# First block: the second transpose of the retention result moved ahead of one branch product, in a single-core fp32 two-block kernel

## The chip, the cores and the metric

One core of a Trainium2 chip (trn2) runs the whole program once. The metric is the device time of that execution in microseconds (us). A core has TensorE (PE, matrix products), VectorE (DVE), ScalarE (ACT), GpSimd (POOL) and SyncE (SP), which here only issues transfers. Each engine works through its own instruction list in order; they meet at semaphores.

## The reference, cut to what matters

Two blocks, one after the other, each of two layers, over 256 tokens of width 1024. The first block's layer:

```python
h = rms_norm(x, norm_g)
proj = h @ w_in                       # 8704 columns
a = diff_attention(...) * silu(az)    # branch 0, 512 wide
c = short_conv(...)     * silu(cz)    # branch 1
r = retention(...)      * silu(rz)    # branch 2
merged = sum(g[:, :, i] * (branches[i] @ w_branch[i]) for i in range(3))
x = x + merged @ w_out
```

The second block (feed-forward, a mixer with two attentions and a delta rule, feed-forward, twice) is in the program too, but the change leaves its order alone.

## The kernel before, in words

**Precision.** All large products are fp32 in effect. A weight piece of 128 x 2048 values (1 MB) is parted in a high and a low half: ACT copies `ring` to `ring_high` (line 1797), then DVE writes the rest, `ring` minus `ring_high`, as `ring_low` (line 2110). The activations are parted in the same way. PE then multiplies high by high, high by low and low by high (`in_parts`, lines 1162 to 1164), so each tile costs three matmuls.

**Rooms.** A loaded piece goes to one of four slots of `ring`, its high half to one of three slots of `ring_high`. A piece can be parted only once it has landed and PE is done with the piece that had its `ring_high` slot before. The transfers depend on the `ring` slots alone.

**Order.** `STEPS1` is the list of steps of a layer of the first block. Every engine takes the steps in which it has a part, in this order. ("d", o) is a product of the input projection. ("br", i, jp) is a quarter of the product of branch i (24 matmuls of 256 columns). ("RF2", t) is, on DVE, the last two operations on the retention result of token tile t (scale, then times silu), and `o_done` tells of it. ("RFT", t) turns it: PE waits for `o_done`, transposes four 128 x 128 tiles into bank 6, and ACT reads them out to `rT`. ("bs", 2) parts `rT` in a high half (ACT) and a low half (DVE, `scratch_low`, 128x1024), and the first product of branch 2 waits for the low half:

```python
                    if jp == 0:
                        pe.wait_ge(*branch_low(L, BRANCH_TURN[i]))
                    arrived(L, piece)
```

Projection and branch products take banks 0 to 3 in turn. After each branch product DVE multiplies the bank with the gate (line 2113); for branch 0 POOL adds that to the sum `hT` (line 2695), for branch 2 DVE does. ("ms", jp) parts a quarter of the merged sum, high half on ACT, low half on DVE (`hT_low`, 128x512). ("wo", q) for q = 0, 1 and then ("wl", i, a) are the output product: "wo" pieces 0 and 1 are used whole (24 matmuls of 512 columns each), pieces 2 and 3 by four quarters i, piece 2 + a by ("wl", i, a). ("wl", 0, 0) waits for the low half of "wo" piece 2 and of the merged quarter 2, ("wl", 0, 1) for those of piece 3 and quarter 3. The ("wl", ...) steps are interleaved with the start of the next layer.

**The planner.** The class `Plan` gives each piece its slots and puts the ("split", piece) steps into the list, at the earliest step behind which its slot is free. Slots go round in turn, but one of three must be skipped once, so that the turn ends where it began. Where the skip lies is chosen by a score: the sum over all pieces of 1 over the number of list positions between the freeing of the slot and its next use, rounded to one decimal; of equals the first in its list of ways is taken. The score changes when any step of the list moves.

Of the kernel before, what the change touches and what calls it, by code (L numbers as in the profile page):

```python
# [106 lines left out]
def quarters(last):  # L107
    return [last + (i, a) for i in range(4) for a in range(2)]
# [23 lines left out]
def attention_slots(kind):  # L132
# [29 lines left out]
    + merge([("RI", 0), ("RK",), ("RI", 1), ("RV", 0), ("RC",), ("RF", 0), ("RV", 1),  # L162
             ("RF2", 0), ("RF", 1)], dense(29, 34))
    + [("br", 1, 0), ("bs", 0)] + [("br", 1, jp) for jp in range(1, 4)]
    + [("br", 0, 0), ("RFT", 0), ("RF2", 1), ("br", 0, 1), ("br", 0, 2), ("RFT", 1), ("bs", 2), ("br", 0, 3)]
    + LAST_BRANCH + quarters(("wl",))
)

# [2721 lines left out]
```

How the kernel before makes its waits and increments, by code:

```python
            def __call__(self, eng, ins):  # L996
                self.n += 1
                ins.then_inc(self.sem, 1)
                eng.wait_ge(self.sem, self.n)
# [34 lines left out]
        @block.sync  # L1034
# [50 lines left out]
            def load_gain(last):  # L1085
                sp.wait_ge(*drained(last, ("br", 2, 3)))
                gain = a["final_norm_2" if last[0] else "final_norm_g"]
                sp.dma_start(final_gain, gain.partition_broadcast(P)).then_inc(end_gain.sem, 16)
# [1 line left out]
            def head(L, before):  # L1090
                for n, piece in enumerate(PLANS[L[0]].pieces[:RING]):
                    if n == 0 and L == (1, 0):
                        load_gain(before)
                    if n == 2 and before is None:
                        load_parameters()
                    if before is not None:
                        plan = PLANS[before[0]]
                        sp.wait_ge(*used(before, plan.last_in_slot[PLANS[L[0]].slot[piece]]))
                    load(L, piece)
# [1 line left out]
            def tail(L):  # L1102
                plan = PLANS[L[0]]
                for piece in plan.pieces[RING:]:
                    sp.wait_ge(*used(L, plan.before_in_slot[piece]))
                    load(L, piece)
# [12 lines left out]
                    load_gain(last)  # L1119
            for i in range(4):
                t, cols = i // 2, slice(512 * (i % 2), 512 * (i % 2) + 512)
                sp.wait_ge(end_out.sem, i + 1)
                sp.dma_start(out[0, t * P:(t + 1) * P, cols], xe[:, t, cols]).then_inc(stored, 16)
            sp.wait_ge(stored, 16 * 4)
```

## Time and profile before

| what | value |
|---|---|
| median of 3 runs | 2030.4 us (2030.25 to 2030.7) |
| the profiled execution's own time | 2031.24 us |
| its span, first to last instruction | 2029.5 us |
| PE busy | 1994.5 us, 98% |
| DVE, ACT, POOL busy | 65%, 45%, 9% |
| granted TensorE clock | 1.000 |

The profiled execution spends 1.7 us outside the span. PE is busy in nearly every microsecond, so the kernel's time is PE's instructions plus the few places where PE stands still; a busy PE is not one at its peak, since its matmuls overlap.

### The profile page before, as it was taken

What the parts mean: (1) busy time and instruction counts of PE and PEld (TensorE: products, weight loads), DVE (VectorE), ACT (ScalarE), POOL (GpSimd) and SP (SyncE); (2) the same over time, 40 slices, a digit from 0 to 9 for tenths busy, and PEclk for the clock granted to TensorE, in tenths of its full rate; (3) what the DMA queues carried; (4) which work ended last, traced back from release to release, by engine and by line L of the source; (5) the groups of instructions that cost most, each with busy time, mean ns of one, the idle gap of its engine ahead of it and who ended that gap; (6) DMA issues with size and microseconds to landing.
All of it is one profiled execution on the core that took longest, in us unless ns stands there. A gap on an engine that the chain in (4) does not pass through costs nothing.

```text
span 2029.5 us, 36575 instructions
## 1 busy us (share of the span) xinstructions
PE 1994.5 (98%) x15633; PEld 1804.7 (89%) x15633; DVE 1320.9 (65%) x1730; ACT 905.0 (45%) x1282; POOL 184.1 (9%) x218
## 2 busy tenths in 40 slices
PE   8999999999999999999999999999999999999998
PEld 8999989999988889799988888888897999888887
DVE  6675674675787777755436776777778545358765
ACT  4544344444454446553424344444455544324443
POOL 1200004000100001301111000000013001110000
PEclk9999999999999999999999999999999999999999
DMA  7455445555556655333324566566653333235664
GB/s 245 153 171 175 164 154 182 166 167 166 185 159 192 194 175 156 119 105 116 115 77 153 182 192 187 167 188 193 194 166 115 119 112 105 84 130 176 192 187 135
DMA packets 347737, 320.42 MB, mean 158 GB/s; under 512 B 9932, under 2 KB 317753, under 8 KB 347577
## 3 DMA queue, kind: packets, MB, share of 16 engines
q1 hardware_dynamic: 347576, 318.08, 49.5%
q8 instruction: 125, 2.05, 0.4%
q14 instruction: 36, 0.29, 0.0%
HBM read 317.01 MB, written 1.05 MB: 157 GB/s over the span
## 4 chain that ended last, share of the span: by engine, by line
PE 92%; DVE 4%; ACT 2%; issue 1%; DMA 1%; POOL 0%; SPq 0%; DVEq 0%; POOLq 0%; ACTq 0%
PE banks L1162 17%; PE banks L1163 17%; PE banks L1164 17%; PE banks L1261 15%; PE banks L1260 7%; PE banks L1157 6%; PE banks L1658 3%; PE banks L1183 3%; DVE ring_low L2110 2%; ACT ring_high L1797 1%; PE banks L1263 1%; PE banks L1387 1%; PE banks L1374 1%; DMA ring<-in_ffn_w_gu 1%; DVE scratch L2110 1%
## 5 line engine op out<-in xcount | busy, mean ns | idle before, releaser
L2110 DVE TENSOR_TENSOR ring_low<-ring,ring_high 128x2048 fp32r<-128x2048 f32 x284 | 657.4, 2317 | 339.8 <-ACT ring_high L1797 338.3
L1797 ACT ACTIVATE ring_high<-ring 128x2048 fp32r<-128x2048 f32 x284 | 542.5, 1911 | 223.5 <-PE banks L1164 166.9
L1261 PE MATMUL banks<-hT_low,ring_high 128*128 128x512 f32 x1344 | 465.6, 397 | 1.6 <-DVE ring_low L2110 1.6
L1162 PE MATMUL banks<-hT_low,ring_high 128*128 128x256 f32 x1408 | 408.9, 290 | 0.0
L1164 PE MATMUL banks<-hT_low,ring_low 128*128 128x256 f32 x1408 | 398.0, 283 | 0.0
L1163 PE MATMUL banks<-hT_low,ring_high 128*128 128x256 f32 x1344 | 380.3, 283 | 0.0
L1260 PE MATMUL banks<-hT_low,ring_low 128*128 128x256 f32 x1176 | 328.2, 279 | 0.0
L1261 PEld LDWEIGHTS banks<-hT_low,ring_high 128*128 128x128 f32 x1344 | 243.0, 188 | 49.1 <-DVE ring_low L2110 2.4
L1162 PEld LDWEIGHTS banks<-hT_low,ring_high 128*128 128x128 f32 x1408 | 269.6, 191 | 5.2 <-issue 2.6
L1164 PEld LDWEIGHTS banks<-hT_low,ring_low 128*128 128x128 f32 x1408 | 269.5, 191 | 0.0
L1163 PEld LDWEIGHTS banks<-hT_low,ring_high 128*128 128x128 f32 x1344 | 257.6, 192 | 0.6 <-issue 0.5
L1797 ACT ACTIVATE scratch<-banks 128x256 f32<-128x256 f32 (+3 forms) x302 | 129.2, 449 | 269.5 <-PE banks L1164 94.5
L1162 PE MATMUL banks<-ring_high,hT_low 128*128 128x256 f32 (+1 forms) x768 | 236.1, 307 | 4.0 <-DVE ring_low L2110 4.0
L1163 PE MATMUL banks<-ring_low,hT_low 128*128 128x256 f32 (+1 forms) x768 | 231.1, 301 | 0.0
L1164 PE MATMUL banks<-ring_high,hT_low 128*128 128x256 f32 (+1 forms) x768 | 231.1, 301 | 0.0
L1260 PEld LDWEIGHTS banks<-hT_low,ring_low 128*128 128x128 f32 x1176 | 221.8, 189 | 7.5
L1162 PEld LDWEIGHTS banks<-ring_high,hT_low 128*128 128x128 f32 x768 | 147.0, 191 | 10.5 <-DVE ring_low L2110 4.7
L1164 PEld LDWEIGHTS banks<-ring_high,hT_low 128*128 128x128 f32 x768 | 146.7, 191 | 5.2
L1163 PEld LDWEIGHTS banks<-ring_low,hT_low 128*128 128x128 f32 x768 | 146.9, 191 | 4.4
L1995 ACT ACTIVATE gates<-gates 128x256 f32<-128x256 f32 x84 | 35.1, 418 | 247.3 <-DVE gates L2385 247.3
L1162 PE MATMUL banks<-ring_high,gates_low 128*128 128x512 f32 x352 | 138.2, 393 | 0.0
L1163 PE MATMUL banks<-ring_low,gates_low 128*128 128x512 f32 x352 | 137.1, 390 | 0.0
(216 smaller groups left out, 2605.6 us busy)
## 6 DMA issues: line engine op xcount, KB each, us to landing
ring<-in_w_in SPq DMA_DIRECT2D x122, 1024.0 KB, 5.0
ring<-in_ffn_w_gu SPq DMA_DIRECT2D x176, 512.0 KB, 4.8
ring<-in_ffn_w_down SPq DMA_DIRECT2D x44, 1024.0 KB, 4.9
ring<-in_w_out SPq DMA_DIRECT2D x16, 1024.0 KB, 5.0
ring<-in_w_branch SPq DMA_DIRECT2D x12, 1024.0 KB, 4.9
ring<-in_w_br_mla SPq DMA_DIRECT2D x4, 1024.0 KB, 5.2
ring<-in_w_br_fox SPq DMA_DIRECT2D x4, 1024.0 KB, 5.2
ring<-in_w_br_dn SPq DMA_DIRECT2D x4, 1024.0 KB, 5.0
```

The source lines that it names most:

```text
L1157: mm = pe.matmul(acc, lhs(k), rhs(k), start=(k == 0), stop=(k == n_k - 1))
L1162: pe.matmul(acc, lhs[0], rhs[0], start=start, stop=False)
L1163: pe.matmul(acc, lhs[0], rhs[1], start=False, stop=False)
L1164: return pe.matmul(acc, lhs[1], rhs[0], start=False, stop=stop)
L1183: return pe.transpose(out_, in_, ident[0:n, 0:n])
L1260: pe.matmul(acc[:, SEQ:], lhs(k)[1], h_high[:, k], start=False, stop=False)
L1261: mm = pe.matmul(acc[:, :], lhs(k)[0], h_pair[:, :, k], start=(k == 0), stop=(k == KD - 1))
L1263: pe.matmul(acc[:, SEQ:], lhs(k)[1], h_high[:, k], start=False, stop=False)
L1658: mm = pe.matmul(at(acc, n, HD)[chunk], left(n)[chunk], right(n)[chunk], start=True, stop=True)
L1797: return act.activation(o, i, ACT.Copy)
L1995: act.activation(to, src, ACT.Tanh, scale=0.5).then_inc(ffn_tanh_done.sem, 1)
L2110: return dve.tensor_tensor(o, i0, i1, op)
```

## The change

One line of the order changes: ("RFT", 1) and ("bs", 2) stand ahead of ("br", 0, 2), not behind it.

```diff
     + [("br", 1, 0), ("bs", 0)] + [("br", 1, jp) for jp in range(1, 4)]
-    + [("br", 0, 0), ("RFT", 0), ("RF2", 1), ("br", 0, 1), ("br", 0, 2), ("RFT", 1), ("bs", 2), ("br", 0, 3)]
+    + [("br", 0, 0), ("RFT", 0), ("RF2", 1), ("br", 0, 1), ("RFT", 1), ("bs", 2), ("br", 0, 2), ("br", 0, 3)]
     + LAST_BRANCH + quarters(("wl",))
```

The planner reads this list. With the new one the rounded scores tie otherwise, and the skip of the high slots moves from the piece ("in", 28) to the piece ("wo", 1). Slots of `ring`, and with them all transfers, stay as they were, and so do POOL's and SP's lists.

On PE, second layer of the first block, before: the product ("br", 0, 2) ends in banks0, the four transposes follow, then ("br", 0, 3).

```order
3903 L1163 MATMUL banks0<-scratch_low,ring_high 128x256
3904 L1164 MATMUL banks0<-hT_low,ring_low 128x256
3905 L1183 MATMUL banks3<-const,scratch 128x128 x4
3906 L1162 MATMUL banks0<-hT_low,ring_high 128x256
3907 L1163 MATMUL banks0<-scratch_low,ring_high 128x256
```

The same place in the changed kernel: the transposes follow ("br", 0, 1), which ends in banks1.

```order
3879 L1163 MATMUL banks1<-scratch_low,ring_high 128x256
3880 L1164 MATMUL banks1<-hT_low,ring_low 128x256
3881 L1183 MATMUL banks3<-const,scratch 128x128 x4
3882 L1162 MATMUL banks0<-hT_low,ring_high 128x256
3883 L1163 MATMUL banks0<-scratch_low,ring_high 128x256
```

They moved ahead by the 24 matmuls of one branch product.

On DVE, first layer, from the low half of the weights ("br", 2, 1) to the end of the output product's partings. The row scratch_low is the low half of ("bs", 2); hT_low are ("ms", 0) to ("ms", 3). Before:

```order
L2113 SCALAR_TENSOR_TENSOR scratch<-gates,banks1 128x512
L2110 TENSOR_TENSOR hT<-hT,scratch 128x512
L2110 TENSOR_TENSOR ring_low<-ring,ring_high 128x2048
L2110 TENSOR_TENSOR hT_low<-hT,hT_low 128x512
L2113 SCALAR_TENSOR_TENSOR scratch<-gates,banks0 128x512
L2110 TENSOR_TENSOR hT<-hT,scratch 128x512
L2110 TENSOR_TENSOR hT_low<-hT,hT_low 128x512
L2113 SCALAR_TENSOR_TENSOR scratch<-gates,banks0 128x512
L2110 TENSOR_TENSOR hT<-hT,scratch 128x512
L2110 TENSOR_TENSOR ring_low<-ring,ring_high 128x2048 x2
L2110 TENSOR_TENSOR hT_low<-hT,hT_low 128x512 x2
L2110 TENSOR_TENSOR ring_low<-ring,ring_high 128x2048
```

In the changed kernel the first of these ring_low rows, ("wo", 1), is gone from there and stands with ("wo", 2) and ("wo", 3) ahead of ("ms", 2) and ("ms", 3):

```order
L2113 SCALAR_TENSOR_TENSOR scratch<-gates,banks1 128x512
L2110 TENSOR_TENSOR hT<-hT,scratch 128x512
L2110 TENSOR_TENSOR hT_low<-hT,hT_low 128x512
L2113 SCALAR_TENSOR_TENSOR scratch<-gates,banks0 128x512
L2110 TENSOR_TENSOR hT<-hT,scratch 128x512
L2110 TENSOR_TENSOR hT_low<-hT,hT_low 128x512
L2113 SCALAR_TENSOR_TENSOR scratch<-gates,banks0 128x512
L2110 TENSOR_TENSOR hT<-hT,scratch 128x512
L2110 TENSOR_TENSOR ring_low<-ring,ring_high 128x2048 x3
L2110 TENSOR_TENSOR hT_low<-hT,hT_low 128x512 x2
L2110 TENSOR_TENSOR ring_low<-ring,ring_high 128x2048
```

On ACT, first layer, the same place and the place of the old skip, as a difference. ring_high rows are high halves of weights, gates rows read products ("d", 26) and ("d", 27), the scratch row between them is ("FT", "diff", 0), hT_low rows are the high halves of ("ms", ...).

```order
-L1896 ACTIVATE gates<-banks1 128x512
-L1797 ACTIVATE ring_high<-ring 128x2048
-L1797 ACTIVATE scratch<-banks3 128x4x128
-L1896 ACTIVATE gates<-banks1 128x512
-L1797 ACTIVATE ring_high<-ring 128x2048 x2
+L1797 ACTIVATE ring_high<-ring 128x2048
+L1896 ACTIVATE gates<-banks1 128x512
+L1797 ACTIVATE ring_high<-ring 128x2048
+L1797 ACTIVATE scratch<-banks3 128x4x128
+L1896 ACTIVATE gates<-banks1 128x512
+L1797 ACTIVATE ring_high<-ring 128x2048
```

There ("in", 28) and ("in", 29) are parted one product sooner. In the output product ACT now parts ("wo", 1) behind ("br", 2, 3), where ("wo", 2) stood, and ("wo", 2) and ("wo", 3) together behind ("wo", 0), where ("wo", 3) stood alone.

## Rows read from the trace of the kernel before

**Rows 1.** The page: span, and busy time by engine.
```profile
span 2029.5 us, 36575 instructions
PE 1994.5 (98%) x15633; PEld 1804.7 (89%) x15633; DVE 1320.9 (65%) x1730; ACT 905.0 (45%) x1282; POOL 184.1 (9%) x218
```
**Rows 2.** Timeline of PE, branch products: start, duration, line, tiles, idle before, releaser.
```profile
249.46 0.28 PE L1164 MATMUL banks<-hT_low,ring_low 128*128 128x256 f32 x1
249.57 0.28 PE L1162 MATMUL banks<-hT_low,ring_high 128*128 128x256 f32 x1
...
255.54 0.28 PE L1164 MATMUL banks<-hT_low,ring_low 128*128 128x256 f32 x1
256.80 0.38 PE L1162 MATMUL banks<-scratch_low,ring_high 128*128 128x256 f32 x1 [0.98 <-DVE scratch_low L2110]
257.02 0.28 PE L1163 MATMUL banks<-scratch_low,ring_high 128*128 128x256 f32 x1
...
532.83 0.38 PE L1162 MATMUL banks<-scratch_low,ring_high 128*128 128x256 f32 x1 [0.98 <-DVE scratch_low L2110]
```
**Rows 3.** Timeline of DVE, 249 to 257 us, first layer.
```profile
249.24 1.67 DVE L2110 TENSOR_TENSOR scratch<-scratch 128x512 f32<-128x512 f32 x1
...
251.78 3.22 DVE L2110 TENSOR_TENSOR ring_low<-ring,ring_high 128x2048 fp32r<-128x2048 f32 x1 [0.28 <-ACT ring_high L1797]
...
255.53 1.21 DVE L2110 TENSOR_TENSOR scratch_low<-scratch,scratch_low 128x1024 fp32r<-128x1024 f32 x1
```
**Rows 4.** Timelines of DVE and POOL: one such DVE operation alone, and POOL's add.
```profile
231.70 0.69 DVE L2110 TENSOR_TENSOR scratch<-scratch 128x512 f32<-128x512 f32 x1
...
248.68 1.68 POOL L2695 TENSOR_TENSOR hT<-hT,scratch 128x512 f32<-128x512 f32 x1 [8.95 <-DVE scratch L2113]
```
**Rows 5.** Timeline of ACT, 249 to 255 us.
```profile
249.83 1.92 ACT L1797 ACTIVATE ring_high<-ring 128x2048 fp32r<-128x2048 f32 x1 [2.28 <-PE banks L1164]
253.03 0.60 ACT L1797 ACTIVATE scratch<-banks 128x512 f32<-128x512 f32 x1 [1.27 <-PE banks L1183]
253.66 1.06 ACT L1797 ACTIVATE scratch_low<-scratch 128x1024 fp32r<-128x1024 f32 x1
```
**Rows 6.** Timelines of DVE, ACT and PE around the old skip.
```profile
191.51 0.69 DVE L2110 TENSOR_TENSOR scratch<-scratch 128x512 f32<-128x512 f32 x1
194.76 4.49 DVE L2110 TENSOR_TENSOR ring_low<-ring,ring_high 128x2048 fp32r<-128x2048 f32 x2 [2.56 <-ACT ring_high L1797]
...
192.83 3.71 ACT L1797 ACTIVATE ring_high<-ring 128x2048 fp32r<-128x2048 f32 x2
```
**Rows 7.** Timeline of PE, output product: last of ("wo", 0), first of ("wl", 0, 0).
```profile
273.34 0.39 PE L1164 MATMUL banks<-ring_high,hT_low 128*128 128x512 f32 x1
...
279.01 0.39 PE L1162 MATMUL banks<-ring_high,hT_low 128*128 128x512 f32 x1
```
**Rows 8.** Timelines of ACT and DVE, output product.
```profile
273.83 1.92 ACT L1797 ACTIVATE ring_high<-ring 128x2048 fp32r<-128x2048 f32 x1 [3.54 <-PE banks L1164]
...
270.78 2.28 DVE L2110 TENSOR_TENSOR ring_low<-ring,ring_high 128x2048 fp32r<-128x2048 f32 x1
275.77 2.29 DVE L2110 TENSOR_TENSOR ring_low<-ring,ring_high 128x2048 fp32r<-128x2048 f32 x1 [2.71 <-ACT ring_high L1797]
277.98 1.29 DVE L2110 TENSOR_TENSOR hT_low<-hT,hT_low 128x512 fp32r<-128x512 f32 x2
```
**Rows 9.** Timelines of PE and DVE, from the first block to the second.
```profile
560.25 0.39 PE L1164 MATMUL banks<-ring_high,hT_low 128*128 128x512 f32 x1
561.67 0.63 PE L1183 MATMUL banks<-const,scratch 128*128 128x128 f32 x4 [1.03 <-DVE scratch L2110]
565.36 0.38 PE L1203 MATMUL banks<-const,stat_all 128*128 128x128 f32 x2
...
562.16 0.69 DVE L2110 TENSOR_TENSOR scratch<-x,scratch 128x512 f32<-128x512 f32 x1
```
**Rows 10.** Timeline of PE, a step from the first layer to the second.
```profile
295.90 0.35 PE L1203 MATMUL banks<-const,stat_all 128*128 128x128 f32 x1 [0.76 <-POOL stat_all L2695]
```

## The prediction

> **What bounds the kernel now.** I read the page first: PE is busy 1994.5 of 2029.5 us [rows 1], so only what lengthens or shortens PE's own list, or a place where PE stands still, can move the time. Then I went through PE's timeline in both layers of the first block and looked at the distance from one start to the next: within a branch product it is 0.12 us (249.46 to 249.57), and a larger distance is a stall. Between the projection and the output product there is one in each layer: the last matmul of ("br", 0, 3) starts at 255.54 and the first of ("br", 2, 0) at 256.80, 1.26 us later, so 1.14 us are lost, and the row names the low half of the parted retention result, DVE's scratch_low, as what ended the wait [rows 2]. The second layer is the same 276.03 us later (532.83) [rows 2]. That is what the moved steps feed. Last I followed DVE, POOL and ACT around both places that the new order touches. The transposes, the product and the merge all need no transfer that the change moves.
>
> **The old wait, step by step.** DVE's second operation of ("RF2", 1) ends at 249.24 + 1.67 = 250.91 [rows 3]. Before, PE was then in the middle of ("br", 0, 2), and met the transposes only after it. ACT read them from 253.03 for 0.60 and parted the high half from 253.66 for 1.06, to 254.72 [rows 5]; DVE had the low half from 255.53 to 256.74 [rows 3], and PE started 0.06 us behind it. After a wait PE's second start comes 0.22 us behind the first and not 0.12 [rows 2], so 0.10 more is lost. The whole removable cost is 1.24 us a layer.
>
> **The transposes one product sooner.** In the new order PE meets them behind ("br", 0, 1), whose last matmul starts at 249.46; the next instruction would start at 249.57 [rows 2]. But they need ("RF2", 1), ready at 250.91. With 0.05 us for the signal PE starts them at 250.96: 1.39 us lost, and about 0.05 for the slow start. That is a new wait, on the producer of the result. Queued behind it on PE are ("br", 0, 2), ("br", 0, 3) and all of branch 2.
> Is the old wait then really gone? ("br", 2, 0) would be met at 255.54 + 0.12 + 1.44 = 257.10. The transposes end about 251.6. ACT is parting ("br", 2, 1) until 249.83 + 1.92 = 251.75 [rows 5], then reads (0.60) and parts (1.06), to about 253.45. DVE is busy with that piece's low half until 251.78 + 3.22 = 255.00 [rows 3], then makes the low half of the result in 1.21: 256.2. That is 0.9 us ahead of PE. The gate multiplication of ("br", 0, 2) now stands behind it on DVE, ending near 256.8; its bank is claimed again only four products later. So the old wait goes and the new one stays: +1.44 - 1.24 = **+0.2 us a layer**.
>
> **Why the producer is late.** The DVE operation of 1.67 us is the same kind that takes 0.69 us at 231.70 [rows 4]. The difference of 0.98 us is spent while POOL adds the product ("br", 0, 0) to the sum, 248.68 to 250.36 [rows 4]. Nothing ahead of that point moves, so I keep 1.67.
> The Trainium skill, SBUF — State Buffer, "Who interferes with whom", says that a DVE instruction with two SBUF inputs and a GpSimd instruction that reads SBUF exclude one another, and that the one issued second fully blocks. By that rule the 1.67 recurs, since POOL's add still comes first; without it the operation would take 0.69, the new wait would be 0.46 and a layer would gain 0.8 us. The trace agrees with the rule here: DVE ends 0.55 us after POOL does.
>
> **The skip of the high slot, old place.** Before, two weights were parted behind ("d", 27): 3.71 us on ACT and 4.49 on DVE [rows 6]. Now they come one product apart. PE had no stall there before, so nothing is to be won. Could it lose? ("in", 29)'s low half now stands ahead of ("F2", "diff", 1) in DVE's list, where ("in", 28)'s was; it takes the same turn at the same time, behind ("d", 26), and DVE's last operation of that step still ends at 191.51 + 0.69 = 192.20 [rows 6]. Zero.
>
> **The skip, new place.** This is the costly part. ("wo", 1) takes the high slot that ("br", 2, 1) has until ("br", 2, 3) ends, ("wo", 2) that of ("wo", 0), and ("wo", 3) stands behind it. First ("wo", 1): it takes the turn that ("wo", 2) had, whose low half ran from 270.78 to 273.06 [rows 8]; shifted by 0.2 it ends at 273.3, and PE wants it at 273.34 + 0.23 + 0.2 = 273.8 [rows 7]. No stall, with 0.5 us to spare.
> Then the pair. Before, ACT started ("wo", 3) at 273.83, when ("wo", 0) had ended, DVE ended its low half at 275.77 + 2.29 = 278.06 and the merged quarters 2 and 3 from 277.98 on, 1.29 us for both, the first of them at 278.67 [rows 8]. PE wanted quarter 2 at 279.01 [rows 7]: covered by 0.34 us. Now two pieces stand between the end of ("wo", 0) and the quarters. ACT starts at 274.03, DVE at 275.97, and a pair takes DVE 4.49 us [rows 6], to 280.46 (ACT's second high half is ready at 277.7, in time; the slot's transfer too, since it is issued at the end of ("br", 2, 3) as before). The low half of quarter 2 overlaps that end by 0.08 and takes 0.69: 281.07. PE could start ("wl", 0, 0) at 279.21 and starts at 281.12. **1.92 us lost, 2.0 with the slow start.** ("wl", 0, 1) needs quarter 3 at 281.7 and is met at 282.6: covered. The skip costs what one low half costs DVE (4.49 - 2.29 = 2.20) less the old cover of 0.34.
>
> **What of it reaches the end.** First layer: 0.2 + 2.0 = +2.2. The step to the next layer has one stall of 0.92 us at 295.90, 0.76 of it idle [rows 10]; it hangs on the last quarter's product through the addition to x, the square sums and the root, so it moves along with PE and gives nothing back. Second layer: +2.2 too up to ("wl", 1, 1). There PE waited before: that product's last matmul starts at 560.25, the transposes would follow at 560.49 and start at 561.67, 1.18 us late, since DVE still had the split of the feed-forward weight and the additions to do [rows 9]. That DVE work hangs on PE only by the end of ("wo", 0), which is 0.2 us late, so a PE that is 2.2 us late finds it done, and 1.18 plus 0.1 for the slow start are absorbed: +0.95. But now DVE's second addition waits for PE: the second scaled x, ended at 562.16 + 0.69 = 562.85 before [rows 9], ends at 564.3. The square sum, variance and root behind it bring the row of roots, which PE took at 565.36 [rows 9], to about 566.6 where PE would be at 566.3: 0.3 given back, and about 0.1 won again later. Second layer: +1.2.
>
> **Sum.** 2.2 + 1.2 = **+3.4 us**. The profiled execution ran 2031.24 us, 1.7 outside its span; it would come to 2034.6. It is 0.8 above the median of 2030.4, and the difference is applied to the median: **2033.8 us**, 0.17% slower. From no change a measurement here can tell about 0.2%, 4.1 us.
>
> **The rivals.**
> *The change does what it seems to do.* The old wait goes and no new one comes: -2 x 1.14 = -2.3 us, 2028.1. It needs ("RF2", 1) to be done by 249.6, 1.3 us sooner than its row ends, and the pair of splits to be hidden as well. Nothing in the rows supports the first. Chance 0.06. It decides for a gain as soon as the two new waits together stay below the old 1.24.
> *Only the turn counts.* The tail is hidden, because DVE or ACT has room that I mis-see: 2 x 0.2 = +0.4, 2030.8. Against it is the cover of 0.34 beside an added 2.2. Chance 0.08.
> *The DVE operation is not held up by POOL this time* (0.69 for 1.67): about -0.8 - 0.8 + 2.0 + 0.7 = about +1.5 with the tail, 2031.9. Against it: POOL's add starts ahead as before. Chance 0.06.
> *Nothing is absorbed between the blocks:* 2 x 2.2 = +4.4, 2034.8, and slower by 0.22%. For it speaks that the additions and square sums there hang on PE as well as on DVE, and that one of them already binds in my sum. Chance 0.15. *More than that* (the splits or gate multiplications meet POOL's adds, up to 1 us each, or the slow starts add up; up to 2037): 0.05.
> Forecast, 2032.8 to 2034.4: 0.60.
>
> **How the numbers follow.** The unknowns are small: the overlap of DVE's operations, the absorbed share, the POOL meeting. Leaving out the two lowest cases (0.14) and the highest (0.05), the range is 2031.5 to 2035.4. Faster by over 0.2% (below 2026.3) no case reaches: 0.02. Slower by over 0.2% (above 2034.5) come the last two cases, 0.20. The rest is within: 0.78.
>
> **What would show it.** In the changed profile PE idles before the L1183 transposes near 251.0 and 527.0, about 1.2 to 1.4 us, released by DVE's scratch L2110; the idle of 0.98 before L1162 on scratch_low is gone. PE idles about 1.7 us near 281.1 before L1162 on hT_low, released by DVE hT_low. DVE has two ring_low in a row there, 4.5 us, ahead of the two hT_low. The idle of 1.03 us at 561.67 is gone or small. The stall at 295.90 stands with the same idle, 2.2 us later. I am wrong if DVE's operation at 249.24 ends sooner, if PE runs into ("wl", 0, 0) without a wait, or if a wait appears behind ("br", 0, 3).

## The result

| kernel | median us | lowest to highest | runs |
|---|---|---|---|
| before | 2030.78 | 2030.25 to 2032.1 | 8 |
| after | 2037.48 | 2034.99 to 2042.06 | 8 |

The ratio of after to before is 1.0032, 95% interval 1.0023 to 1.0041: the change made the kernel 6.7 us slower. The forecast was +3.4 us, with 2035.4 as the upper end of its range. Both of the waits that it named are there, at the predicted places and of the predicted length. What it lacks is a second cost that stands behind the longer of them: TensorE's clock falls.

**The page of after** (the profiled execution: 2042.06 us, the slowest of the eight) answers to [rows 1].

```profile
span 2040.3 us, 36575 instructions
PE 2001.8 (98%) x15633; PEld 1809.4 (89%) x15633; DVE 1320.2 (65%) x1730; ACT 905.1 (44%) x1282; POOL 181.7 (9%) x218
```

The count of instructions is that of before, and DVE, ACT and POOL are busy for as long as before, within 2.4 us. Yet PE, with the same count of 15633 matmuls, is busy 7.3 us longer. Waits alone can't do that, since a waiting PE isn't busy. This line is the first sign that matmuls themselves ran slower somewhere.

**Timeline of PE in after** (start, duration, line, tiles, idle before and releaser): the transposes of both layers, then the step from ("wo", 0) to ("wl", 0, 0) of both. It answers to [rows 2] and [rows 7].

```profile
251.51 0.28 PE L1164 MATMUL banks<-hT_low,ring_low 128*128 128x256 f32 x1
253.00 0.66 PE L1183 MATMUL banks<-const,scratch 128*128 128x128 f32 x4 [1.21 <-DVE scratch L2110]
...
533.07 0.44 PE L1183 MATMUL banks<-const,scratch 128*128 128x128 f32 x2 [1.24 <-DVE scratch L2110]
...
281.10 0.39 PE L1164 MATMUL banks<-ring_high,hT_low 128*128 128x512 f32 x1
283.34 0.47 PE L1162 MATMUL banks<-ring_high,hT_low 128*128 128x512 f32 x1 [1.85 <-DVE hT_low L2110]
283.65 0.39 PE L1163 MATMUL banks<-ring_low,hT_low 128*128 128x512 f32 x1
...
284.57 0.63 PE L1164 MATMUL banks<-ring_high,hT_low 128*128 128x512 f32 x1
285.00 0.63 PE L1162 MATMUL banks<-ring_high,hT_low 128*128 128x512 f32 x1
285.43 0.63 PE L1163 MATMUL banks<-ring_low,hT_low 128*128 128x512 f32 x1
...
563.41 0.47 PE L1162 MATMUL banks<-ring_high,hT_low 128*128 128x512 f32 x1 [1.85 <-DVE hT_low L2110]
```

The transposes start 1.49 us behind the last matmul where 0.12 is a step: 1.37 us lost, 1.39 forecast ahead of the slow start. Ahead of ("wl", 0, 0) it is 283.34 - 281.10 - 0.23 = 2.01 us, 1.92 forecast; the step behind it is 0.31 us and not 0.23, so with the slow start it is 2.09 us, 2.0 forecast. The wait of 0.98 us on scratch_low [rows 2] is gone. Now read on behind 283.34: from 284.57 on the start of one 512-column matmul is 0.43 us behind the one before, where 0.23 is the usual step [rows 7]. Nothing is waited for there. The matmuls are longer.

**DVE and ACT in after**, the same two places, timeline. It answers to [rows 3], [rows 5] and [rows 8].

```profile
251.29 1.65 DVE L2110 TENSOR_TENSOR scratch<-scratch 128x512 f32<-128x512 f32 x1
...
253.83 3.23 DVE L2110 TENSOR_TENSOR ring_low<-ring,ring_high 128x2048 fp32r<-128x2048 f32 x1 [0.29 <-ACT ring_high L1797]
256.98 1.21 DVE L2110 TENSOR_TENSOR scratch_low<-scratch,scratch_low 128x1024 fp32r<-128x1024 f32 x1
272.65 2.29 DVE L2110 TENSOR_TENSOR ring_low<-ring,ring_high 128x2048 fp32r<-128x2048 f32 x1 [0.60 <-ACT ring_high L1797]
278.10 4.49 DVE L2110 TENSOR_TENSOR ring_low<-ring,ring_high 128x2048 fp32r<-128x2048 f32 x2 [3.16 <-ACT ring_high L1797]
282.51 1.29 DVE L2110 TENSOR_TENSOR hT_low<-hT,hT_low 128x512 fp32r<-128x512 f32 x2
...
276.15 3.72 ACT L1797 ACTIVATE ring_high<-ring 128x2048 fp32r<-128x2048 f32 x2 [3.53 <-PE banks L1164]
```

DVE's chain is the forecast one: two ring_low in a row for 4.49 us, then the quarters; quarter 2, the first of the two, takes 0.68 us and is done at 283.19, 0.15 us ahead of PE's start at 283.34. The operation ahead of the transposes again takes 1.65 us.

**The windows of after** show what the timeline hints at. Columns: the stretch, its length, busy time of PE, PEld, DVE, ACT and POOL, then PEclk, the granted clock as a share of 2.4 GHz, DMA share and GB/s.

```profile
20.00:240.00 220.00, 219.06 (x1818) 214.69 (x1818) 138.78 (x195) 102.04 (x131) 23.61 (x28) 1.00 0.52 170
253.00:283.00 30.00, 28.49 (x196) 26.26 (x196) 22.31 (x20) 13.63 (x12) 3.84 (x3) 1.00 0.52 175
284.50:287.90 3.40, 3.40 (x9) 2.65 (x9) 1.60 (x2) 0.00 (x0) 0.00 (x0) 0.50 0.43 151
288.20:292.00 3.80, 3.80 (x20) 3.12 (x19) 1.57 (x3) 1.28 (x4) 0.00 (x0) 1.00 0.02 4
564.40:567.80 3.40, 3.40 (x10) 2.62 (x9) 1.66 (x1) 0.00 (x0) 0.00 (x0) 0.50 0.59 178
827.20:830.60 3.40, 3.40 (x7) 1.99 (x8) 3.24 (x10) 0.60 (x3) 1.24 (x1) 0.51 0.63 222
```

Behind each of the two waits ahead of ("wl", 0, 0) lies a stretch of 3.4 us at 0.50, the lower level of 1.2 GHz. PE counts as busy all through it, and at half clock does in 3.4 us the work of 1.7, so each stretch costs 1.7 us: eight steps of 0.43 us where 0.23 is usual make 1.6. The profiled execution of before ran these places, and all but its last few microseconds, at 1.00. After the transposes' wait (253.00 to 283.00) the clock stays at 1.00. The profiled execution of after has another such stretch from 18.3 us on, behind a wait of 1.90 us for the first weights. The stretch at 827 lies in the second block, and no idle is recorded right ahead of it:

```profile
824.50:827.10 2.60, 2.60 (x23) 2.12 (x22) 0.85 (x2) 1.51 (x3) 1.57 (x1) 1.00 0.43 98
```

PE counts as busy there throughout, mostly with small matmuls (128x8 and 128x128), so in this one case the clock fell with no wait before it.

**Where the 10.8 us between the two spans went** (2040.3 to 2029.5), from the starts of the same PE instructions in both traces: 295.90 in before is 301.97 in after (+6.1), 573.08 is 582.05 (+9.0), 824.04 is 834.68 (+10.6).

| stretch | longer by us |
|---|---|
| start to 105 us, ahead of all that changed: the first weights came later, and the clock fell once | 2.1 |
| layer 1, new waits less the old one (1.43 + 2.09 - 1.24) | 2.3 |
| layer 1, half clock behind the wait | 1.7 |
| layer 2, the same waits | 2.3 |
| layer 2, half clock | 1.7 |
| step to the second block, absorbed | -1.0 |
| half clock at 827 us | 1.7 |
| rest | 0.1 |
| sum, by rounding 0.1 too high | 10.9 |

The row of the start is not the change's: up to 105 us both kernels run the same instructions. The eight executions of after bear the division out by themselves. Seven have a mean granted clock of 0.996 to 0.998 and took 2036.56 to 2042.06 us. The one with 1.000 took 2034.99, which is 4.2 us above the median of before and inside the forecast range. A mean that rounds to 1.000 leaves room for 2 us at half clock at most, so in that execution neither wait brought a stretch of 3.4 us.

### The profile page after: what moved, and what is told of

Same layout as the page of the kernel before. It is cut to its first block, busy times and chain, and to the rows that moved or that the text cites. A ratio compares the mean times of both kernels' runs of the same rounds, so it can differ in the third digit from the quotient of the medians.

```text
span 2040.3 us, 36575 instructions
## 1 busy us (share of the span) xinstructions
PE 2001.8 (98%) x15633; PEld 1809.4 (89%) x15633; DVE 1320.2 (65%) x1730; ACT 905.1 (44%) x1282; POOL 181.7 (9%) x218
## 4 chain that ended last, share of the span: by engine, by line
PE 91%; DVE 4%; ACT 2%; DMA 1%; issue 1%; POOL 0%; SPq 0%; DVEq 0%; POOLq 0%; ACTq 0%
PE banks L1162 17%; PE banks L1164 17%; PE banks L1163 17%; PE banks L1261 15%; PE banks L1260 7%; PE banks L1157 6%; PE banks L1658 3%; PE banks L1183 3%; DVE ring_low L2110 2%; ACT ring_high L1797 1%; PE banks L1263 1%; DVE scratch L2110 1%; DMA ring<-in_w_in 1%; PE banks L1387 1%; PE banks L1374 1%
## 5 line engine op out<-in xcount | busy, mean ns | idle before, releaser
L1162 PE MATMUL banks<-ring_high,gates_low 128*128 128x512 f32 x352 | 138.1, 392 | 0.0
L1164 PE MATMUL banks<-ring_high,gates_low 128*128 128x512 f32 x352 | 137.0, 389 | 0.0
```

Source lines behind the costliest of these rows:

```text
L1162: pe.matmul(acc, lhs[0], rhs[0], start=start, stop=False)
L1164: return pe.matmul(acc, lhs[1], rhs[0], start=False, stop=stop)
```

## The experiments

Each was timed beside runs of the kernel before on the same chip; that one's median was 2030.68 us (24 runs) beside the first four and 2030.89 (27 runs) beside the last four. The skip of the planner is held in place by two lines in `Plan.places`, which give the position of the piece at which it may lie (28 is the old place, ("in", 28); 41 the new one, ("wo", 1)). The inserted lines shift the line numbers in these traces by up to 3.

| label | median us | lowest to highest | runs | ratio to before, 95% |
|---|---|---|---|---|
| e1_turn_only | 2031.65 | 2030.64 to 2034.56 | 11 | 1.0005 (0.9996 to 1.0014) |
| e2_skip_only | 2036.85 | 2035.47 to 2038.26 | 8 | 1.0028 (1.0018 to 1.0039) |
| e3_merge_first | 2031.29 | 2030.29 to 2033.44 | 11 | 1.0002 (0.9993 to 1.0011) |
| e4_filled | 2039.66 | 2038.68 to 2041.02 | 5 | 1.0043 (1.0030 to 1.0057) |
| e5_filled8 | 2034.76 | 2034.39 to 2036.45 | 11 | 1.0021 (1.0012 to 1.0029) |
| e6_result_sooner | 2028.43 | 2027.69 to 2029.59 | 11 | 0.9988 (0.9979 to 0.9997) |
| e7_pool_after | 2029.41 | 2028.85 to 2031.13 | 11 | 0.9994 (0.9985 to 1.0003) |
| e8_longer_wait | 2039.31 | 2039.10 to 2041.04 | 5 | 1.0045 (1.0032 to 1.0057) |

### The two halves of the change apart

**e1_turn_only**: the new order, the skip held at its old place.

```diff
+            if not blk and n == HIGHS:
+                return placed(pieces, n, range(28, 30), 1)[2]
             ways = ways if blk else ways[::-1]
```

> The changed order, but the planner's skip of a high slot is held at the piece (in, 28), where it lay before. The whole computation is done. Theory A (two new waits of fixed size, and a clock that falls only behind the 2 us wait in the output product): PE idles about 1.2 us ahead of the transposes in each layer, no wait ahead of (wl, 0, 0), granted clock 1.00 as before, time +0.2 to +0.6 us over before. Theory B (the clock fell in the changed kernel for a reason that has nothing to do with its waits, or already because of the transposes' wait): clock stretches at 0.5 here too, time +3 or more. Theory C (the turn itself is a gain, all loss is the skip's): time -2 us.

**e2_skip_only**: the order of before, the skip held at the new place. Against the kernel before:

```diff
+            if not blk and n == HIGHS:
+                return placed(pieces, n, range(41, 43), 1)[2]
```

> The order of before, but the skip of the high slot held at (wo, 1), where the changed kernel has it. The whole computation is done. Theory A: the old wait of 1.14 us ahead of branch 2 stays, PE idles about 1.8 us ahead of (wl, 0, 0) in both layers, and stretches of about 3.4 us at half clock follow it in part of the executions, as in the changed kernel (1.7 us each); time +3.0 us without them, +4 to +6.5 with them, so nearly all of the changed kernel's +6.7. Theory B: no stretch at half clock, +3.0. Rival in which the transposes' new wait is what matters: time within 1 us of before.

The timeline of PE in e1_turn_only at the transposes:

```profile
250.69 0.55 PE L1185 MATMUL banks<-const,scratch 128*128 128x128 f32 x3 [1.21 <-DVE scratch L2112]
```

Its windows, from ahead of the transposes to behind the output product, and in the second block:

```profile
240.00:300.00 60.00, 58.03 (x401) 53.44 (x401) 47.43 (x50) 26.19 (x28) 6.62 (x6) 1.00 0.52 173
...
1562.10:1565.50 3.40, 3.40 (x18) 3.40 (x17) 3.37 (x3) 0.00 (x0) 3.32 (x3) 0.50 0.00 0
```

And the windows of e2_skip_only, ahead of ("wl", 0, 0) and behind it in layer 1, then behind it in layer 2:

```profile
278.00:281.90 3.90, 2.05 (x10) 1.42 (x9) 3.90 (x4) 2.14 (x2) 0.00 (x0) 1.00 0.47 152
282.00:285.40 3.40, 3.40 (x10) 2.63 (x9) 1.73 (x2) 0.00 (x0) 0.00 (x0) 0.50 0.35 123
285.40:290.00 4.60, 4.60 (x25) 3.79 (x25) 1.79 (x4) 1.45 (x4) 0.11 (x1) 1.00 0.01 4
...
561.90:565.30 3.40, 3.40 (x10) 2.62 (x9) 1.84 (x2) 0.00 (x0) 0.00 (x0) 0.50 0.40 121
```

The first, e1_turn_only, has the idle of 1.21 us at the transposes, and in the output product neither a wait nor half clock (in the second block it has one such stretch). The second, e2_skip_only, which turns the result where before did, idles for half of the stretch ahead of ("wl", 0, 0), and has the stretches at 0.50 behind it. The turn alone gives +1.0 us (too little to tell from no change), the skip alone +6.2, together 7.2; the change has +6.7. So the skip makes the loss, and the line of the diff that a reader looks at first makes little of it. All eight executions of e2_skip_only have a mean clock of 0.997 or 0.998.

### Is it the wait ahead of ("wl", 0, 0), or the moved slots?

**e3_merge_first**: the changed kernel with the skip at its new place, but ("ms", 2) and ("ms", 3) ahead of ("wo", 0), so that the quarters don't queue behind the pair of splits on DVE.

```diff
-    + LAST_BRANCH + quarters(("wl",))
+    + [s for s in LAST_BRANCH if s not in (("wo", 0), ("wo", 1), ("ms", 2), ("ms", 3))]
+    + [("ms", 2), ("ms", 3), ("wo", 0), ("wo", 1)] + quarters(("wl",))
+            if not blk and n == HIGHS:
+                return placed(pieces, n, range(41, 43), 1)[2]
```

> The changed kernel, skip at (wo, 1) as there, but the merged quarters 2 and 3 are parted ahead of (wo, 0), so that DVE does them before the pair of weight halves. The whole computation is done. Theory A: the wait ahead of (wl, 0, 0) is gone though the pair of splits is as late as before it, because the quarters no longer stand behind them; a stall of at most 0.1 us ahead of (wl, 0, 1); clock 1.00; time +0.2 to +0.8 us over before. Rival (PE waits for the weights themselves, not for the quarters): the wait stays, above 1 us, time +3 or more.

The timeline of PE in e3_merge_first, around the end of ("wo", 0):

```profile
280.16 0.39 PE L1166 MATMUL banks<-ring_low,hT_low 128*128 128x512 f32 x1
280.39 0.39 PE L1167 MATMUL banks<-ring_high,hT_low 128*128 128x512 f32 x1
280.61 0.45 PE L1165 MATMUL banks<-ring_high,hT_low 128*128 128x512 f32 x1
280.90 0.39 PE L1166 MATMUL banks<-ring_low,hT_low 128*128 128x512 f32 x1
```

Steps of 0.23 us with one of 0.29: no wait. The time is 0.6 us above before, which is no measurable difference. The moved slots by themselves cost nothing that can be measured; the wait that they make is the loss. The windows of e3_merge_first, the first layer from the transposes on and the second block's stretch at half clock:

```profile
240.00:300.00 60.00, 58.03 (x400) 53.27 (x400) 47.84 (x50) 25.98 (x28) 6.62 (x6) 1.00 0.51 174
...
834.80:838.20 3.40, 3.40 (x19) 3.40 (x18) 3.37 (x3) 0.00 (x0) 3.16 (x2) 0.50 0.00 0
```

Both output products run at 1.00. The fall at 834.8 will be of use below.

### Does the clock make the part that the waits don't?

**e4_filled** and **e5_filled8**: the changed kernel, with matmuls on constants (17 or 8 of 128x128) ahead of ("wl", 0, 0), written to a free bank that nobody reads. PE then computes where it waited; the wait itself stays as long.

```diff
+                if i == a == 0 and L[0] == 0:
+                    pe.wait_ge(*drained(L, ("br", 2, 3)))
+                    for _ in range(8):
+                        pe.matmul(bank_of(L, ("br", 2, 3))[:, 0:P], ident, ident, start=True, stop=True)
                 if i == 0:
                     arrived(L, ("wo", 2 + a))
```

> The changed kernel with 17 matmuls of constants (128 x 128, results unused, about 1.9 us of PE) ahead of (wl, 0, 0) in both layers of the first block, in the time in which PE waits. The real products start no sooner. Theory A: the clock fell because PE idled there; filled, it stays at 1.00 around 281 and 557 us and the time falls from +6.7 to about +3.4 us (up to +4 if the filling ends late). Theory B: the stretches at half clock stay and so does the time, +6 to +7.

> As the filled kernel before it, with 8 matmuls of constants in place of 17: each takes PE two passes of 0.11 us (34 rows in 3.96 us there), so 8 take about 1.8 us and should end when PE's wait does. The real products start no sooner than in the changed kernel. Theory A (the clock falls because PE idles about 2 us ahead of (wl, 0, 0), and that costs 1.7 us a layer): no stretch at half clock near 284 and 564 us, time +3.2 to +4.2 us over before. Theory B (the clock's fall is not that wait's): +6 to +7.

e4_filled missed: its 17 matmuls took two passes each, 34 in the trace, and lasted past the wait's end. The timeline of PE:

```profile
278.91 3.96 PE L1347 MATMUL banks<-const 128*128 128x128 f32 x34
282.62 0.48 PE L1162 MATMUL banks<-ring_high,hT_low 128*128 128x512 f32 x1
```

The step is 282.62 - 278.91 = 3.7 us where the wait was 2.0, so a layer has 1.7 us of filling that nothing wanted, as much as a fall of the clock costs. Its time therefore decides nothing. Its clock does say something: with no idle left ahead of ("wl", 0, 0) it stays at 1.00 in the output product, here of layer 1, and in layer 2 alike.

```profile
276.00:290.00 14.00, 14.00 (x82) 12.18 (x81) 9.71 (x9) 5.84 (x8) 0.00 (x0) 1.00 0.37 130
```

e5_filled8 was made to fit. Its timeline of PE:

```profile
278.89 0.40 PE L1164 MATMUL banks<-ring_high,hT_low 128*128 128x512 f32 x1
279.12 1.95 PE L1347 MATMUL banks<-const 128*128 128x128 f32 x16
281.13 0.47 PE L1162 MATMUL banks<-ring_high,hT_low 128*128 128x512 f32 x1
```

Its windows, around the output product of each layer:

```profile
276.00:290.00 14.00, 13.95 (x74) 11.69 (x73) 10.67 (x10) 6.06 (x8) 0.56 (x1) 1.00 0.39 133
556.00:570.00 14.00, 13.89 (x74) 11.40 (x73) 11.73 (x16) 6.25 (x13) 1.09 (x2) 1.00 0.34 103
```

The product still starts 2.0 us late (281.13 - 278.89 - 0.23), but the clock is 1.00 on both sides of it in both layers, and the kernel is 2.7 us faster than the change alone, though it computes more: 2034.76 for 2037.48. It stands 3.9 us above before. That is the price of the waits by themselves, and the forecast gave +3.4 for them. The two stretches at half clock cost 3.4 us if both come in an execution; 2.7 is what their absence brought in the medians. The 95% intervals of the two kernels overlap (1.0012 to 1.0029 and 1.0023 to 1.0041), but all 11 executions of e5_filled8 (up to 2036.45) lie below seven of the eight of after (from 2036.56), and the eighth is the one at a clock of 1.000.

**e8_longer_wait**: the kernel before, whose old wait ahead of ("br", 2, 0) is lengthened. DVE squares the retention result twice more into a scratch tile ahead of the low half of ("bs", 2); the values are used nowhere. It asks whether a long wait lets the clock fall at another place too.

```diff
             def split_branch(L, i):
                 dve.wait_ge(*branch_high(L, BRANCH_TURN[i]))
+                if i == 2:
+                    for _ in range(2):
+                        link(tt(r_sq, r_o[:, 1], r_o[:, 1], ALU.mult))
```

> The kernel before, with two extra DVE operations (squares of a dead array, 0.72 us each) ahead of the low half of the retention result, so that the old wait of PE ahead of (br, 2, 0) grows from 1.14 to about 2.6 us in both layers. The result is unchanged. If an idle of this length lets the clock fall wherever it lies: a stretch at half clock behind it in each layer, time +2.9 plus 3.4, about +6.3. If the fall belongs to the output product (its kind of matmul, or the traffic there) and not to the length of the idle: clock 1.00 around 257 and 533 us, time +2.9.

The timeline of PE and DVE:

```profile
256.25 0.28 PE L1164 MATMUL banks<-hT_low,ring_low 128*128 128x256 f32 x1
259.91 0.58 PE L1162 MATMUL banks<-scratch_low,ring_high 128*128 128x256 f32 x1 [3.39 <-DVE scratch_low L2110]
...
256.24 2.36 DVE L2110 TENSOR_TENSOR scratch<-scratch 128x512 f32<-128x512 f32 x2
```

The windows of the two stretches at half clock, one in each layer:

```profile
259.00:265.80 6.80, 5.89 (x27) 5.89 (x28) 4.02 (x4) 0.00 (x0) 3.26 (x1) 0.50 0.28 114
542.30:545.70 3.40, 3.40 (x18) 3.40 (x17) 1.65 (x2) 0.00 (x0) 2.63 (x1) 0.51 0.00 0
```

The wait grew from 1.14 to 3.54 us a layer, more than meant, since the two operations took 2.36 us and not twice 0.69 (a POOL addition ran beside them). The clock fell in both layers, for twice as long in the first, where it fell at 259.0, still within the wait and 0.9 us ahead of PE's restart. The waits are 2 x 2.4 = 4.8 us longer and the kernel 8.4 (2039.31 to 2030.89): the rest is of the size that stretches at half clock make. So it isn't a matter of the output product.

The same profile also has a wait of nearly 2 us with no fall behind it, for the first weights. The timeline of PE there, and the window behind it:

```profile
17.31 0.39 PE L1162 MATMUL banks<-ring_high,hT_low 128*128 128x256 f32 x1 [1.86 <-DVE ring_low L2110]
...
17.30:24.00 6.70, 6.69 (x56) 6.69 (x57) 5.49 (x6) 3.03 (x3) 0.00 (x0) 1.00 0.33 95
```

In after the wait at this place is 1.90 us, and there the clock fell.

### What the moved turn could have had

**e6_result_sooner**: the skip at its old place, ("RF2", 1) two products sooner, ("RFT", 0) ahead of ("br", 0, 0), and the turn one product sooner again.

```diff
-    + [("br", 1, 0), ("bs", 0)] + [("br", 1, jp) for jp in range(1, 4)]
-    + [("br", 0, 0), ("RFT", 0), ("RF2", 1), ("br", 0, 1), ("RFT", 1), ("bs", 2), ("br", 0, 2), ("br", 0, 3)]
+    + [("br", 1, 0), ("bs", 0), ("br", 1, 1), ("br", 1, 2), ("RF2", 1), ("br", 1, 3)]
+    + [("RFT", 0), ("br", 0, 0), ("RFT", 1), ("bs", 2), ("br", 0, 1), ("br", 0, 2), ("br", 0, 3)]
+            if not blk and n == HIGHS:
+                return placed(pieces, n, range(28, 30), 1)[2]
```

> Skip held at (in, 28); on top of the change the retention result itself is made sooner: (RF2, 1) behind (br, 1, 2), the transposes behind (br, 1, 3) and (br, 0, 0). The whole computation is done. Theory A (the turn failed as a gain because it was moved ahead of its producer): no wait at the transposes and none ahead of (br, 2, 0), RF2's second operation back at 0.69 us because POOL has not begun to add, time -2.0 to -2.6 us against before. Rival (a wait of this size is always moved and never won, because DVE's list is what ends last): within 0.6 us of before.

**e7_pool_after**: e1_turn_only, and POOL starts branch 0's first addition only when the retention result is done.

```diff
                 if n < 4:
                     return
+                if n == 4 and L[0] == 0:
+                    pool.wait_ge(*o_done(L, 4))
                 pool.wait_ge(*drained(L, ("br", i, jp)))
```

> As the turn-only kernel (skip at (in, 28)), but POOL begins the first addition of branch 0 only when (RF2, 1) is done. The whole computation is done. If POOL's addition is what stretches DVE's operation: it takes 0.69 us and not 1.67, the new wait at the transposes falls from 1.36 to about 0.4 us, and the time is 1.5 to 2 us below the turn-only kernel, about 1 us below before. If the operation is long for another reason: both unchanged, time as the turn-only kernel, +1.

The timeline of DVE in e6_result_sooner:

```profile
244.43 0.68 DVE L2112 TENSOR_TENSOR scratch<-scratch,stat 128x512 f32<-128x512 f32 x1
245.15 0.69 DVE L2112 TENSOR_TENSOR scratch<-scratch 128x512 f32<-128x512 f32 x1
```

The timeline of DVE, POOL and PE in e7_pool_after:

```profile
249.02 0.69 DVE L2112 TENSOR_TENSOR scratch<-scratch 128x512 f32<-128x512 f32 x1
...
249.79 2.54 POOL L2697 TENSOR_TENSOR hT<-hT,scratch 128x512 f32<-128x512 f32 x2 [10.28 <-DVE scratch L2112]
...
249.77 0.44 PE L1185 MATMUL banks<-const,scratch 128*128 128x128 f32 x2 [0.25 <-DVE scratch L2112]
```

In e7_pool_after the same DVE operation at the same time takes 0.69 us where it took 1.65, with nothing changed but POOL's start; and the wait at the transposes falls from 1.36 to 0.40 us. So POOL's addition is what held DVE up. By the medians the kernel is 2.2 us faster than e1_turn_only, but the two were timed beside different sets of runs and their intervals overlap, so how much of that is real isn't shown. The Trainium skill, SBUF — State Buffer, "Who interferes with whom", describes such an exclusion of a DVE instruction with two SBUF inputs and a GpSimd instruction that reads SBUF; these rows agree.

In e6_result_sooner the result is ready 5 us sooner (at 245.84, and at 250.91 in before), and no addition of POOL runs beside it. Neither the transposes nor ("br", 2, 0) wait, and the kernel is 2.5 us faster than before (2028.43 to 2030.89): the two old waits of 1.14 us. It is faster than both kernels, before and after. The moved turn was worth having, once its producer had moved and the skip had not.

## Why the prediction was wrong

**"The old wait, step by step"**: right. The idle of 0.98 us on scratch_low is gone in after; e2_skip_only, where the transposes stand as before, has it again (at 256.35).

**"The transposes one product sooner"**, 1.39 us and 0.05 for the slow start: right, 1.37 in layer 1 and 1.40 in layer 2, and 0.06 for the start. The sum of old and new, +0.2 a layer, is within the interval of e1_turn_only (+1.0 us, not to be told from zero).

**"Why the producer is late"**, 1.67 us: right, 1.65, and e7_pool_after shows the cause.

**"The skip of the high slot, old place"**, zero: PE waits nowhere there in after.

**"The skip, new place"**, 1.92 us and 2.0 with the slow start: right, 2.01 and 2.09 in layer 1, and the same within 0.01 in layer 2, by the chain described. e3_merge_first takes the wait away and with it the loss.

**"What of it reaches the end"**: its balance of waits is right. The stall of 1.18 us at the step between the blocks is gone, a new one of 0.22 us lies behind it: 1.0 absorbed, as forecast. The stall at 295.90 kept its length. The sum of the waits, +3.4 us, measured +3.9 in e5_filled8.

**The step that failed** is the one that ends in "First layer: 0.2 + 2.0 = +2.2" and is carried into the "Sum". It priced a wait of 2 us at its length, and took every matmul behind it at its old pace; of a slow start it allowed 0.08 us. In fact TensorE's clock fell to 0.50 about a microsecond behind PE's restart and stayed there for 3.4 us, which costs 1.7 us more. No term and no rival had that; the unlikely "more than that" ended at 2037, and for other reasons. Behind the wait of 1.37 us in the same layer there was no fall, so what a wait costs is not in proportion to its length. With the clock the sum would have been 3.4 + 2 x 1.7 = +6.8; +6.7 was measured. That they meet to 0.1 us is in part luck: the interval of the ratio spans +4.7 to +8.3 us, and the medians of both kernels hold stretches at half clock elsewhere.

The kernel before has such executions too. Of its 51 beside the experiments 23 have a mean clock of 0.998 or less, at least 6 us at half clock, and the program's end, with PE done, takes at most 4.1 of them in any of the ten profiles. Those at 1.000 had a median of 2030.23 us (9 of 24) and 2030.65 (7 of 27), those at 0.998 one of 2031.68 and 2031.15. A median of before is therefore no time at full clock.

The rows of before held a warning only in part. PE idles for 1.70 us ahead of 834.13 and of 1561.59 in the trace of before, with the clock at 1.00 behind both; nothing in that trace shows a fall in the middle.

```profile
834.13 0.39 PE L1162 MATMUL banks<-ring_high,hT_low 128*128 128x256 f32 x1 [1.70 <-DVE ring_low L2110]
```

But e3_merge_first has a fall at 834.8, e1_turn_only one at 1562.1 and e4_filled one at 841.0, right behind these very idles. In the ten profiles such an idle stands twenty times, and a fall lies behind three of them. Behind an idle of this length, then, the clock falls in some executions and not in others. That was not to be read from the one trace at hand; a rival with the clock in it would still have been in place, since the forecast put waits of 1.92 us into the output product, and the longest behind which that trace shows the clock, once the weights have come, are 1.70. The Trainium skill, TensorE: Matmul & The Clock Gate, "What's actually happening", says that the clock follows how busy PE has been; the rows agree in that PE's pauses are what preceded the falls in the output product: a gap of 1.85 us was followed by a fall in four of four cases, in two profiled executions.

What stays open: from which length on a wait brings the fall, and what else decides. Idles of 0.98 to 1.33 us had none behind them in any of the profiles, those of 1.70 in 3 of 20 cases, those of 1.85 in the output product in all four. But these four are two pairs, each within one execution. One execution of after had a mean clock of 1.000 with the same waits in it, and the idle of 1.86 us at 17.31 in e8_longer_wait had no fall behind it. So a wait of this length brings the fall often and not always. Whether the fall at 827 us in after has to do with the change at all wasn't shown; nor was it settled whether e1_turn_only's +1.0 is more than the 0.4 that its waits make, since its interval holds both.

## What to carry to other kernels

A wait of TensorE that nears 2 us in an otherwise dense stretch may cost nearly twice its length, because the clock can fall behind it. Forecast such a wait with and without 1.7 us more, and look at the granted clock of the stretch behind it, and at the mean clock of every execution, before believing a sum of gaps; a rise of PE's busy time at the same count of instructions is the sign. And when a planner reads the list that is edited, what it does in answer may weigh more than the edit: hold its choice fixed and time the two apart. An instruction moved ahead is worth what its producer allows, so the producer goes first.

## What was not expected of the hardware

- The stretches at 1.2 GHz were nearly all of one length, 3.4 us, and one of twice that behind an idle of 3.39 us (e8_longer_wait). Those behind an idle began at no fixed distance from PE's restart: most 0.4 to 1.5 us behind it (in after the wait ends at 283.34, the long steps begin at 284.57), the one in e4_filled 0.1 us behind it, and the long one 0.9 us ahead of it, while PE still waited.
- One stretch at 1.2 GHz (827.2 in after) came with no idle of PE recorded right ahead of it.
- Eight small matmuls (1.95 us of work without use) ahead of the product, with the clock at 1.00 behind them in the profile, and the kernel 2.7 us faster by the medians.
- A 128x128 matmul of plain fp32 constants (e4_filled) shows as two rows: 17 instructions gave 34, 3.96 us together, about 0.11 us a row.
